# Expert choice ranks each sequence in two halves on separate partitions and merges the two ranked lists, one of them reversed

## What is computed

```python
def expert_choice(xn, w_router, w_eg, w_eu, w_ed):
    T = B * S
    C = CAPACITY_FACTOR * T // N_EXPERTS
    xt = xn.reshape(T, D)
    aff = jax.nn.softmax((xt @ w_router).astype(jnp.float32), axis=-1)
    gate, idx = lax.top_k(aff.T, C)
    xe = xt[idx]
    h = jax.nn.silu(jnp.einsum('ecd,edf->ecf', xe, w_eg)) * jnp.einsum('ecd,edf->ecf', xe, w_eu)
    ye = jnp.einsum('ecf,efd->ecd', h, w_ed) * gate[..., None].astype(xn.dtype)
    out = jnp.zeros((T, D), xn.dtype).at[idx.reshape(-1)].add(ye.reshape(-1, D))
```

## Time and profile before

| what | value |
|---|---|
| median of 3 runs | 3261.97 us (3261.85 to 3262.48) |
| profiled execution | 3265.93 us |
| its span, by the profile | 3264.1 us |
| PE busy (matmul) | 3080.3 us, 94% |
| DVE busy | 1898.6 us, 58% |
| ACT busy | 1471.7 us, 45% |
| POOL busy | 164.2 us, 5% |
| block with the ranking | about 1184 to 1417 us |
| from the first to the last ranking instruction | 1318.6 to 1416.4 us |

### The profile page before, as it was taken

The page is one execution under the profiler, slowest core; times in us unless marked ns, Lnnn a source line. Parts: engine busy times, 40 slices in busy tenths (PEclk is TensorE's granted clock), DMA queues, the critical chain, the costliest instruction groups (busy, mean ns, idle before and its releaser), DMA issues. The chain is left out here.

```text
span 3264.1 us, 46120 instructions
## 1 busy us (share of the span) xinstructions
PE 3080.3 (94%) x17704; PEld 2751.0 (84%) x17704; DVE 1898.6 (58%) x2801; ACT 1471.7 (45%) x2006; POOL 164.2 (5%) x212
## 2 busy tenths in 40 slices
PE   5999999899999999659999999999999999999993
PEld 4888889855877878549999999999999999999993
DVE  5242332334344343867777777777777777777773
ACT  4232223123333234235655565555555555655552
POOL 0101010000000000010000000001000000000000
PEclk9999999999999999769999999999999999999997
DMA  5222121212333433346777777777767776777664
GB/s 175 80 77 81 66 87 38 92 33 70 96 91 90 129 129 116 110 133 239 241 248 232 238 243 244 232 250 245 242 225 250 247 249 233 246 233 247 233 214 170
DMA packets 470001, 562.71 MB, mean 172 GB/s; under 512 B 14523, under 2 KB 383419, under 8 KB 469788
## 3 DMA queue, kind: packets, MB, share of 16 engines
q1 hardware_dynamic: 459004, 526.15, 47.8%
q0 software_dynamic: 10912, 35.40, 4.3%
HBM read 517.31 MB, written 44.19 MB: 172 GB/s over the span
## 5 line engine op out<-in xcount | busy, mean ns | idle before, releaser
L1550 PE MATMUL ps<-xsplit,wh 128*128 128x384 f32 x4096 | 1168.8, 360 | 2.2 <-DVE xsplit L1646 2.2
L1552 PE MATMUL ps<-xsplit,wl 128*128 128x192 f32 x4096 | 1026.6, 251 | 0.0
L1639 DVE TENSOR_TENSOR wl<-raw,wh 128x2048 fp32r<-128x2048 f32 x384 | 876.9, 2284 | 94.0 <-ACT wh L1596 92.9
L1596 ACT ACTIVATE wh<-raw 128x2048 fp32r<-128x2048 f32 x384 | 734.1, 1912 | 329.3 <-PE ps L1574 303.4
L1552 PEld LDWEIGHTS ps<-xsplit,wl 128*128 128x128 f32 x4096 | 783.9, 191 | 0.6
L1550 PEld LDWEIGHTS ps<-xsplit,wh 128*128 128x128 f32 x4096 | 770.7, 188 | 3.2 <-issue 2.6
L1610 ACT ACTIVATE low<-ps 128x384 f32<-128x384 f32 x256 | 126.0, 492 | 435.4 <-PE ps L1552 435.4
L1655 DVE TENSOR_TENSOR gu<-ps,low 128x384 f32<-128x384 f32 x256 | 142.8, 558 | 220.9 <-ACT low L1610 220.9
L1115 DVE TENSOR_TENSOR glow<-graw,ghigh 128x1024 fp32r<-128x1024 f32 x72 | 88.1, 1225 | 235.6 <-ACT ghigh L1071 235.6
L1569 PE MATMUL ps<-wh,hsplit 128*128 128x512 f32 x512 | 201.0, 392 | 0.0
L1573 PE MATMUL ps<-wh,hsplit 128*128 128x512 f32 x512 | 199.5, 390 | 0.0
(11 more groups left out here) (223 smaller groups left out, 4545.1 us busy)
## 6 DMA issues: line engine op xcount, KB each, us to landing
raw<-in_w_exp_gate_dram SPq DMA_DIRECT2D x128, 1024.0 KB, 5.6
raw<-in_w_exp_up_dram SPq DMA_DIRECT2D x128, 1024.0 KB, 7.8
raw<-in_w_exp_down_dram SPq DMA_DIRECT2D x128, 1024.0 KB, 6.1
graw<-in_w_gate_dram SPq DMA_DIRECT2D x96, 256.0 KB, 2.9
wraw<-in_w_in_dram SPq DMA_DIRECT2D x21, 1024.0 KB, 5.1
graw<-in_w_four_br_dram SPq DMA_DIRECT2D x24, 384.0 KB, 3.5
xin<-in_x_dram SPq DMA_DIRECT2D x12, 512.0 KB, 3.8
xres<-in_x_dram SPq DMA_DIRECT2D x12, 512.0 KB, 3.5
```

What stands on the lines that cost most here:

```text
L1550: pe.matmul(ps[:, bank, 0:2 * CAP], wh[:, q % AHEAD, tile], xsplit[:, k, :, :].rearrange("p s t -> p (s t)"), start=k == 0, stop=False)
L1552: mm = pe.matmul(ps[:, bank, CAP:2 * CAP], wl[:, q % AHEAD, tile], xsplit[:, k, 0, :], start=False, stop=k == KT - 1)
L1596: act.activation(cut_part(wh, q), raw_part(q), ACT.Copy).then_inc(w_high, 1)
L1639: dve.tensor_tensor(cut_part(wl, q), raw_part(q), cut_part(wh, q).bitcast(F32), ALU.subtract).then_inc(w_cut, 1)
```

## The change

The 1024 columns of the prompt are kept as two halves of 512, on partitions 0 to 15 and 32 to 47, the 512 of the sample as two of 256, on partitions 64 to 79 and 96 to 111. `softmax` writes the affinities into the 16 of 112 columns that belong to its half, so that the transpose puts them on these partitions. One round ranks both halves of a sequence at once, over partitions 0 to 47 or 64 to 111; the 16 rows between hold -2. The number of rounds stays: each half gives its own best 128 (or 64), in falling order.

`ranked(s)` copies the values and the numbers of the tokens of both halves to `lists`, the second half's in reverse. PE transposes both (`turn_lists`), ACT copies them from PSUM (`paired`), and DVE takes place by place the larger of the two (`best`): of a falling and a rising list of n values each, the larger of every pair are the n largest of all 2n. The number of the token is picked with `is_ge`, a difference, a product and a sum.

The order by hand changes with it. The 16 prompt rounds are four in each of rows 8 to 11. In row 12, `ranked(0)`, `turn_lists(0)` and `paired(0)` stand behind `turn(11)` and in front of the logits, and `best(0)` behind the softmax and in front of `keep`. `turn_lists(1)`, `paired(1)` and `best(1)` end the block. POOL fills three tiles at its head, and DVE waits for them behind `low_w_out`.

```diff
--- before.py
+++ after.py
...
         junk2 = at("junk2", 172, [P, D])
-        aff = [at("affP", 192, [E, 1024]), at("affS", 196, [E, 512])]
-        vals = [at("valsP", 198, [E, CAPS[0]]), at("valsS", 198.5, [E, CAPS[1]])]
-        idxr = [at("idxrP", 199, [E, CAPS[0]], U32), at("idxrS", 199.5, [E, CAPS[1]], U32)]
-        idxf = [at("idxfP", 200, [E, CAPS[0]]), at("idxfS", 200.5, [E, CAPS[1]])]
-        atok = at("atok", 201, [P, 2, E])
+        aff = at("aff", 192, [P, 512])
+        vals = at("vals", 198, [P, CAPS[0]])
+        idxr = at("idxr", 198.5, [P, CAPS[0]], U32)
+        lists = at("lists", 199, [P, 2, CAPS[0]])
+        atok = at("atok", 201, [P, 2, 112])
+        pairs = at("pairs", 200, [P, 2, 112])
+        pick_f = at("pick_f", 202, [P, 4, E])
...
         r_top, r_idf, r_iT, r_fin = (sem(n) for n in ("r_top", "r_idf", "r_iT", "r_fin"))
+        r_zero, r_pair, r_pick = sem("r_zero"), sem("r_pair"), sem("r_pick")
+        def block_of(t):
+            return (t // 4, t % 4) if t < SEQS[0][1] // P else (2 + (t - 8) // 2, t % 2)
+        def block_rows(b):
+            return slice(32 * b, 32 * b + E)
...
                     sp.wait_ge(r_st[b], 32 * (NT // 2))
+            @block.gpsimd
+            def _(pool):
+                pool.memset(aff[:, :], -2.0).then_inc(r_zero, 1)
+                pool.memset(atok[:, :, :], 0.0).then_inc(r_zero, 1)
+                pool.memset(lists[:, :, :], 0.0).then_inc(r_zero, 1)
...
                         pe.wait_ge(r_aev, t)
-                    pe.transpose(ps[0:E, 5, 0:P], atok[:, t % 2, :], ident[:, :]).then_inc(r_aT, 1)
+                    pe.transpose(ps[0:112, 5, 0:P], atok[:, t % 2, :], ident[:, :]).then_inc(r_aT, 1)
+                def turn_lists(s):
+                    n, cap = (48, 112)[s], CAPS[s]
+                    pe.wait_ge(r_idf, 2 * s + 2)
+                    pe.transpose(ps[0:cap, 6 + s, 0:n], lists[0:n, 0, 0:cap], ident[0:n, 0:n])
+                    pe.transpose(ps[0:cap, 6 + s, 128:128 + n], lists[0:n, 1, 0:cap], ident[0:n, 0:n]).then_inc(r_iT, 1)
...
                         turn(t)
+                    if not row.out:
+                        turn_lists(0)
...
                         turn_aff(t)
-                for s in range(2):
-                    pe.wait_ge(r_idf, s + 1)
-                    cap = CAPS[s]
-                    pe.transpose(ps[0:cap, 6 + s, 0:E], vals[s][:, :], ident[0:E, 0:E])
-                    pe.transpose(ps[0:cap, 6 + s, E:2 * E], idxf[s][:, :], ident[0:E, 0:E]).then_inc(r_iT, 1)
+                turn_lists(1)
...
                                    accum_out=stat[:, 6:7]).then_inc(r_exp, 1)
+                def paired(s):
+                    act.wait_ge(r_iT, s + 1)
+                    if s:
+                        act.wait_ge(r_fin, 1)
+                    act.activation(pairs[0:CAPS[s], :, 0:(48, 112)[s]],
+                                   ps[0:CAPS[s], 6 + s, 0:256].rearrange("p (v n) -> p v n", v=2)[:, :, 0:(48, 112)[s]],
+                                   ACT.Copy).then_inc(r_pair, 1)
...
                         turned(t)
+                    if not row.out:
+                        paired(0)
...
                         softmax(t)
+                paired(1)
...
                 dve.wait_ge(r_g2, 16)
+                dve.wait_ge(r_zero, 3)
...
                         dve.wait_ge(r_aT, t - 1)
-                    dve.tensor_scalar(atok[:, t % 2, :], stat[:, 32 + 16 * (t % 2):48 + 16 * (t % 2)], stat[:, 7:8], None,
+                    cols = block_rows(block_of(t)[0])
+                    dve.tensor_scalar(atok[:, t % 2, cols], stat[:, 32 + 16 * (t % 2):48 + 16 * (t % 2)], stat[:, 7:8], None,
...
                 def keep(t):
-                    s, tile = (0, t) if t < PROMPT_TILES else (1, t - PROMPT_TILES)
+                    b, tile = block_of(t)
                     dve.wait_ge(r_aT, t + 1)
-                    dve.tensor_copy(aff[s][:, tile * P:(tile + 1) * P], ps[0:E, 5, 0:P]).then_inc(r_aev, 1)
+                    dve.tensor_copy(aff[block_rows(b), tile * P:(tile + 1) * P], ps[block_rows(b), 5, 0:P]).then_inc(r_aev, 1)
...
                 def top(s, r):
-                    v = vals[s][:, 8 * r:8 * r + 8]
+                    rows, width = (slice(0, 48), slice(64, 112))[s], SEQS[s][1] // 2
+                    v = vals[rows, 8 * r:8 * r + 8]
...
                         dve.wait_ge(r_top, tops[0])
-                    dve.max(v, aff[s][:, :]).then_inc(r_top, 1)
+                    dve.max(v, aff[rows, 0:width]).then_inc(r_top, 1)
                     dve.wait_ge(r_top, tops[0] + 1)
-                    dve.max_index(idxr[s][:, 8 * r:8 * r + 8], v, aff[s][:, :]).then_inc(r_top, 1)
+                    dve.max_index(idxr[rows, 8 * r:8 * r + 8], v, aff[rows, 0:width]).then_inc(r_top, 1)
                     dve.wait_ge(r_top, tops[0] + 2)
-                    dve.match_replace(aff[s][:, :], v, aff[s][:, :], -1.0).then_inc(r_top, 1)
+                    dve.match_replace(aff[rows, 0:width], v, aff[rows, 0:width], -1.0).then_inc(r_top, 1)
                     tops[0] += 3
-                def as_float(s):
+                def ranked(s):
+                    cap, (base, size) = CAPS[s], SEQS[s]
                     dve.wait_ge(r_top, tops[0])
-                    dve.tensor_scalar(idxf[s][:, :], idxr[s][:, :], float(SEQS[s][0]), None, ALU.add).then_inc(r_idf, 1)
+                    for b in range(2):
+                        rows, order = block_rows(2 * s + b), (slice(0, cap) if b == 0 else slice(cap - 1, None, -1))
+                        first = float(base + b * size // 2)
+                        dve.tensor_copy(lists[rows, 0, 0:cap], vals[rows, 0:cap][:, order])
+                        dve.tensor_scalar(lists[rows, 1, 0:cap], idxr[rows, 0:cap][:, order], first, None, ALU.add).then_inc(r_idf, 1)
+                def best(s):
+                    cap = CAPS[s]
+                    a, b = block_rows(2 * s), block_rows(2 * s + 1)
+                    v, i, w = pairs[0:cap, 0, :], pairs[0:cap, 1, :], pick_f[0:cap, :, :]
+                    dve.wait_ge(r_pair, s + 1)
+                    dve.tensor_tensor(w[:, 0, :], v[:, a], v[:, b], ALU.is_ge).then_inc(r_pick, 1)
+                    dve.tensor_tensor(w[:, 1, :], i[:, a], i[:, b], ALU.subtract).then_inc(r_pick, 1)
+                    dve.tensor_tensor(gate[s][:, :], v[:, a], v[:, b], ALU.max)
+                    dve.wait_ge(r_pick, 3 * s + 2)
+                    dve.tensor_tensor(w[:, 2, :], w[:, 0, :], w[:, 1, :], ALU.mult).then_inc(r_pick, 1)
+                    dve.wait_ge(r_pick, 3 * s + 3)
+                    dve.tensor_tensor(idx[s][:, :], w[:, 2, :], i[:, b], ALU.add).then_inc(r_fin, 1)
...
                             turned(t)
+                    if not row.out:
+                        ranked(0)
                     for t in row.logits:
-                        if not row.out:
-                            top(0, next(rounds))
                         softmax(t)
+                    if not row.out:
+                        best(0)
...
                     elif row.out and row.out[0] > PROMPT_TILES:
-                        for _ in range(2):
+                        for _ in range(3):
                             top(0, next(rounds))
-                for r in rounds:
-                    top(0, r)
-                as_float(0)
...
                     top(1, r)
-                as_float(1)
-                for s in range(2):
-                    cap = CAPS[s]
-                    dve.wait_ge(r_iT, s + 1)
-                    dve.tensor_copy(gate[s][:, :], ps[0:cap, 6 + s, 0:E])
-                    dve.tensor_copy(idx[s][:, :], ps[0:cap, 6 + s, E:2 * E]).then_inc(r_fin, 1)
+                ranked(1)
+                best(1)
```

## The result

The changed kernel took 3247.47 us (median of 5, 3244.04 to 3249.96), the kernel before beside it 3262.36; the ratio is 0.9946, 95% interval 0.9935 to 0.9957, which is 17.6 us less (14.0 to 21.2); the two medians lie 14.9 us apart, inside that interval too. Two more timings of the unchanged text, on other occasions, gave ratios of 0.9944 (0.9929 to 0.9960) and 0.9946 (0.9932 to 0.9960). The prediction was 3243.3 in a range of 3239.5 to 3248.5, 18.7 us less.

A forecast was written before the change was run, and what follows sets the result against it. DVE's ranking chain was taken to end the stage before the experts: 32.0 us removed, 8.9 given back in the last row, 1.4 in the tail, 3 in waits; 3261.97 - 18.7 = 3243.3 us, range 3239.5 to 3248.5.

The forecast's parts named there:

- first MAX8 to the end of the prompt's rounds: DVE's chain through tile rows 8 to 11, all 16 prompt rounds, from 1318.56 to 1371.9 us.
- last row, `ranked(0)` to the sample's first round: Row 12: both `logits` wait behind the prompt's list without cover; 12.6 us, where the same steps took 3.7 of DVE's time.
- eight sample rounds: The sample's ranking on DVE at 256 columns, 1.48 us a round; 11.8 us, ending at 1396.3.
- tail, `ranked(1)` to the end of `best(1)`: The sample's list handling at the block's end: 2.2 us, where it was 0.8 before.
- mark to mark, less than before: From the first ranking instruction to the experts' first ACT instruction; DVE was forecast to end 18.7 us earlier.
- What bounds: DVE's ranking chain ends the stage in front of the PE-bound experts, so what leaves it leaves the total.
- The price of a round: DVE round: 3.87 to 2.27 us at 512 columns, 2.27 to 1.48 at 256, extra partitions free; 32.0 us removed.
- Rival 2: The sample's 256-wide rounds hit a floor and stay at 2.27 us: 6.4 us lost, 3249.7; chance 0.07.
- PE's stalls in front of tiles 10 and 11: PE's waits for `xlow`, 2.78 and 1.81 us before, were to vanish, with tile 11's lower-clock start.
- The margin: `low_mix(11)` on DVE was to end at 1344.4, 1.7 us before PE wants it at 1346.1.
- `ranked`: Its four DVE instructions change partition group each time, costing an estimated 0.2 to 0.3 us more per list.
- What costs nothing: POOL's three memsets, `turn_aff` with 112 weight columns, and the experts' units 1 and 2, loaded earlier, add no time.

The follow-up runs named there:

- e2: Changed kernel with prompt rounds moved back in front of the last row's two softmaxes, the prompt's list handling put later, nothing removed; 3241.10 us, ratio 0.9935.
- e5: Changed kernel with the sample's 8 rounds alone put back to 512 columns; 3253.89 us in its one execution.
- e8: Changed kernel with last row's cover given back, DVE's gaps filled and PE's transpose of tile 9's affinities right behind `logits(10)`; 3237.52 us, ratio 0.9920.

## Why the prediction was right

These are the steps, by the times of the first and of the second trace of the change, against those worked out:

| step | predicted | first trace | second trace |
|---|---|---|---|
| first MAX8 to the end of the prompt's rounds | 53.3 | 53.4 | 52.6 |
| last row, `ranked(0)` to the sample's first round | 12.6 | 12.9 | 12.9 |
| eight sample rounds | 11.8 | 12.1 | 12.1 |
| tail, `ranked(1)` to the end of `best(1)` | 2.2 | 2.3 | 2.3 |
| to the next block's first instruction | 0.6 | 0.6 | 0.6 |
| mark to mark, less than before | 18.7 | 17.9 | 18.7 |

- How exact it was: in part luck. In the second and third trace the 18.7 comes out to a tenth because errors cancel. The first step was forecast 0.7 too long: the additions of tile 9 came 12.1 us behind the first mark, where 13.1 had been worked out from the first trace of before, in which PE had the lower of the two mean clocks (0.65), and the rest of the step took 0.3 more than forecast. The last row, the sample's rounds and the tail were forecast 0.7 too short together. The mechanism stands without that: no step is off by more than 0.7 us in 53.
- What bounds: right. The experts start 1.25 us behind the first instruction of `best(1)` on DVE in every version; what was taken from the chain of the last row, or added to it, was found in the block (e2, e5, e8).
- The price of a round: right at 512 (2.29 on 48 partitions, 2.27 on 16), 0.03 too low at 256. Rival 2's floor would have left the narrow round at 2.27; it took 1.51. The estimate worked out from the Trainium skill ("VectorE: DVE Perf Modes", section on the TRN2 errata), 0.33 us for a 256-wide instruction, doesn't agree with the trace's 0.42. The section itself says that this row of its table comes out too low for a single operation.
- PE's stalls in front of tiles 10 and 11: gone as forecast. The margin worked out as 1.7 was 1.4 (`low_mix(11)` ends at 1341.68, tile 11 starts at 1343.08). The higher clock behind it came too.
- The last row, step by step: `ranked(0)` and hand-over 0.8, for 0.7; transposes 0.45, for 0.5; `logits` 3.59 and 3.56, for 3.4 and 3.57; from `logits(10)` to `logits(11)` 0.76, for 0.7; `best(0)` 0.71, for 0.7. The three `keep`s took 2.14, for 1.9, the largest term that was off. I had said that `turn_aff` with 112 weight columns costs nothing: it takes 0.43 for 0.37, and the copy 0.29 for 0.27.
- `ranked`: I wrote that its four instructions change partition group from one to the next. They don't: there is one change among them, between the halves. The starts are 0.15, 0.24 and 0.14 apart, and the Trainium skill's rule ("VectorE: DVE Perf Modes", section on two Vector instructions with no wait between them) agrees with the trace: the one that changes the group starts 0.24 us behind the one in front, which lasts 0.21, and so behind its end. It costs 0.1 per list, not 0.2 to 0.3.
- What costs nothing: right. POOL's three memsets took 0.53, 0.29 and 0.32 us at 1181.5 to 1182.6, while DVE wanted them at 1193.4. The loads of units 1 and 2 of the experts' weights were issued from 1361.5, and DMA traffic was down to nothing by 1376, 21 us before the experts' start (from 1376 to 1397 the DMA share is 0.00).
- The total: the median of 3247.47 is 4.2 above the forecast. In that execution, which is the traced one, 0.9 of it is in the block, which goes with the clock about the mark. The rest is not in the block. The same program differs by 6.8 us ahead of the block and by 2.2 behind it between its three traces, so 3.3 is within its scatter. The three ratios, 0.9944 to 0.9946, put the gain at 17.6 to 18.3, each within some 4 us; they can't show or exclude a term of 1 us outside the block.

## What to carry to other kernels

Instructions that read a row of n columns on few partitions are shortened by laying the row out as two on twice the partitions; price them by the line through two widths of the same instruction in the trace. When work is taken from a chain, look at what ran on another engine beside it: here a third of the 28.2 us that the block lost in the end, 9.5, came from giving two groups of small matmuls their cover back and closing the gaps, without removing an instruction. And where the gain is a few parts in a thousand, compare the changed stretch from mark to mark in several traces: it repeated within 0.1 us for a given clock, while single executions of the changed kernel lay between 3242.7 and 3250.0.

## What the runs showed of the hardware

- MAX8, FIND_INDEX8 and MATCH_REPLACE8 cost 1.04 ns a column plus some 0.15 us down to 256 columns (0.42, 0.69, 1.22 us for MAX8 at 256, 512, 1024), and almost nothing for three times the partitions: 2.29 for 2.27 a round at 512, 3.89 for 3.87 at 1024.
- 16 matmuls of 16 columns took 1.96 us right behind a filling of PE, and 3.4 with 1.92 us of idle time between; the next 16 took 2.75 and 3.57. In the first case the granted clock fell 0.9 us into the second group, in the other some 0.2 us into the first. Whether these narrow matmuls let it fall, or the idle time in front of them and between them, was not separated.
- The experts' matmuls of 384 columns have two durations, 359 and 364 ns on the mean, in executions of one and the same program. The slow case is a step of 4.64 us and not 4.55, and only in the first expert: in the first trace of the change the steps of the second are 4.55 again. What sets it wasn't tried.
